# A decoder step on one core: 14 of 17 tiles of h transposed by VectorE out of a reload instead of by TensorE, and the first expert block gathered whole and transposed by TensorE

## What is computed

```python
h = layer_norm(ALPHA * x + mix)            # mix = concat(attn, conv) @ w_out + b_out
lg = h @ w_rg                              # 4 groups, top-1
le = h @ w_re                              # 8 experts in the group, top-2
y_moe = sum over 2 experts of gate * (silu(h @ w1[e]) * (h @ w3[e])) @ w2[e]
y = layer_norm(ALPHA * h + y_moe)
```

## Time and profile before

| | us |
|---|---|
| median of 3 runs (lowest, highest) | 1392.42 (1391.33, 1398.35) |
| profiled execution, its own time | 1402.51 |
| its span in the trace | 1400.6 |
| TensorE matmul busy in the span | 1297.0 (93%) |
| VectorE busy | 684.6 (49%) |
| ScalarE busy | 553.8 (40%) |
| GpSimd busy | 477.0 (34%) |
| output stage, first `turn_h` to last | 599.5 to 866.7 |
| expert matmuls | 906.9 to 1337 |

### The profile page before, as it was taken

The page is one execution under the profiler, slowest core; times in us unless marked ns, Lnnn a source line. Parts: engine busy times, 40 slices in busy tenths (PEclk is TensorE's granted clock), DMA queues, the critical chain, the costliest instruction groups (busy, mean ns, idle before and its releaser), DMA issues.

```text
span 1400.6 us, 21325 instructions
## 1 busy us (share of the span) xinstructions
PE 1297.0 (93%) x5597; PEld 624.9 (45%) x5598; DVE 684.6 (49%) x2065; ACT 553.8 (40%) x895; POOL 477.0 (34%) x643
## 2 busy tenths in 40 slices
PE   8999999989999988899999999999999999999910
PEld 3444445556666655355555555433333333333300
DVE  2424343554556555466666665334444444444338
ACT  0000001434345433333334431166655666566544
POOL 5113110000000000355555543344666566666312
PEclk9999999999999998999999999999999999999955
DMA  6364543222211183345555331259989999999676
GB/s 257 107 210 147 168 128 103 95 75 69 76 68 54 53 251 118 116 184 181 181 181 152 121 114 62 76 157 323 324 261 370 345 283 328 332 370 347 188 241 275
DMA packets 81938, 262.31 MB, mean 187 GB/s; under 512 B 13648, under 2 KB 32656, under 8 KB 68726
## 3 DMA queue, kind: packets, MB, share of 16 engines
q1 hardware_dynamic: 64839, 216.56, 42.6%
q0 software_dynamic: 14192, 41.26, 12.3%
q10 hardware_dynamic: 2823, 3.54, 0.8%
HBM read 202.32 MB, written 63.25 MB: 190 GB/s over the span
## 4 chain that ended last, share of the span: by engine, by line
PE 57%; issue 28%; DMA 6%; DVE 4%; ACT 1%; DVEq 1%; SPq 1%; POOL 1%; POOLq 1%; ACTq 0%
PE P L1017 12%; PE bank_S L1039 10%; PE M L1017 6%; PE P L859 5%; PE bank_S L859 4%; PE bank_S L686 4%; DMA work<-conv_rows 3%; PE P L686 3%; PE P L889 3%; PE bank_T L686 2%; PE M L686 2%; PE M L877 1%; PE M L1025 1%; DMA big<-sum_rows 1%; ACT work L1299 1%
## 5 line engine op out<-in xcount | busy, mean ns | idle before, releaser
L1256 ACT ACTIVATE big<-big 128x2048 f32 x78 | 148.9, 1910 | 161.4 <-issue 102.0
L1018 PE MATMUL P<-big,work 128*64 128x512 f32 x416 | 188.0, 595 | 0.0
L1017 PE MATMUL P<-big,work 128*64 x416 | 188.0, 595 | 0.0
L1900 POOL DMA_INDIRECT work<-h_rows,piece_idx x156 | 150.0, 962 | 77.8 <-issue 55.5
L725 PE MATMUL P<-big,work 128*128 128x256 f32 (+1 forms) x512 | 173.7, 496 | 0.0
L1039 PE MATMUL bank_S<-big,work 128*64 x312 | 142.0, 598 | 3.5 <-ACT big L1262 3.1
L1041 PE MATMUL bank_S<-big,work 128*64 128x512 f32 x312 | 142.1, 598 | 0.0
L1837 POOL TENSOR_SCALAR work<-work 128x1 f32<-128x1 f32 (+1 forms) x17 | 3.8, 223 | 373.9 <-DVE work L1447 373.9
L725 PEld LDWEIGHTS P<-big,work 128*128 128x128 f32 x512 | 97.3, 194 | 70.4 <-issue 63.6
L859 PE MATMUL P<-big,work 128*128 128x512 f32 x256 | 116.0, 607 | 3.2 <-DVE work L1478 3.2
L859 PE MATMUL bank_S<-big,work 128*128 128x512 f32 x256 | 113.3, 595 | 0.0
(11 more groups left out here) (304 smaller groups left out, 2278.7 us busy)
## 6 DMA issues: line engine op xcount, KB each, us to landing
big<-in_w SPq DMA_DIRECT2D x96, 1024.0 KB
work<-in_xt_prompt SPq DMA_DIRECT2D x32, 512.0 KB, 3.5
big<-sum_rows SPq DMA_DIRECT2D x16, 520.0 KB, 8.9
big<-in_toe SPq DMA_DIRECT2D x16, 512.0 KB, 3.5
work<-in_x_prompt SPq DMA_DIRECT2D x16, 512.0 KB, 4.3
h_rows<-work SPq DMA_DIRECT2D x16, 512.0 KB
sum_rows<-work SPq DMA_DIRECT2D x16, 512.0 KB
out_y_prompt<-big SPq DMA_DIRECT2D x16, 512.0 KB
```

The source lines that it names most:

```text
L1017: mm(lower, xgT[j][:, k, 0:U], both[:, k], start=(k == 0), stop=(k == KD - 1))
L1018: last = mm(upper, xgT[j][:, k, U:P], w_up[:, k], start=(k == 0), stop=(k == KD - 1))
L1256: fn(w_up.rearrange("p k m f -> p m k f")[:, :, ks, :], src, ACT.Copy).then_inc(s[f"wu{part}_ok"], 1)
L1900: g.indirect_dma_start(xg[j][:, 256 * i:256 * (i + 1)], None, h_pieces, bass.IndirectOffsetOnAxis(ap=piece_idx[:, j, i // 2, i % 2:i % 2 + ...
```

## The change

Tiles 1 to 14 are no longer transposed by TensorE (tiles 0, 15 and 16 still are: `BY_PE`). SyncE, right behind the two stores of h(c-1), waits until both have landed and until `hT` has been written for the tile before, and reads the tile back in four DMAs, each into 32 partitions of a buffer that is free in this stage (`h_parts`, once `ptB`). VectorE turns it in 32x32 squares straight into `hT` at the head of its iteration, ahead of `route_count`. ScalarE's copy goes for these tiles. The first expert block is gathered by one indirect DMA of whole rows, transposed by eight TensorE transposes into `bank_T` and copied by VectorE; `listed(2)` moves behind that copy; `keep_awake(22)` becomes `keep_awake(14)`.

```diff
+        BY_PE = (0, NT - 1, NT)
+        h_parts = flat_ptB
+            def reload_h(c):
+                tile = OUT_IN[c]
+                sp.wait_ge(s[f"h_out{c % 2}"], 32 * (c // 2 + 1))
+                after(sp, s["hT_ev"], c - 1)
+                src = h_dram[P * tile:P * (tile + 1), :].rearrange("(i t) c -> t i c", t=32)
+                for j in range(4):
+                    sp.dma_start(h_parts[32 * j:32 * (j + 1), :].rearrange("p (i c) -> p i c", i=4),
+                                 src[:, :, 256 * j:256 * (j + 1)]).then_inc(s["hp_in"], 16)
...
                     store_h(c - 1)
+                    if c - 1 not in BY_PE:
+                        reload_h(c - 1)
...
-                if 0 <= c - 1 <= NT:
+                if c - 1 in BY_PE:
                     turn_h(c - 1)
...
-            keep_awake(22)
+            keep_awake(14)
...
+            pe.wait_ge(s["xg_in0"], 16)
+            for k in range(KD):
+                last = tr(T8[:, k, :], xg[0][:, k::KD], ident)
+            last.then_inc(s["pe_hT"], 1)
             for b in range(RING):
                 up(b, b, 0)
...
-                after(act, s["pe_hT"], c)
+                after(act, s["pe_hT"], BY_PE.index(c))
...
-                if 0 <= c - 1 <= NT:
+                if c - 1 in BY_PE:
                     turned_h(c - 1)
...
-                        after(v, s["pe_hT"], c - 2)
+                        after(v, s["pe_hT"], sum(x <= c - 2 for x in BY_PE) - 1)
...
+            def flip_h(c):
+                v.wait_ge(s["hp_in"], 64 * c)
+                after(v, s["pe_ro"], c - 1)
+                nc.vector.transpose(hT.rearrange("p k (i t) -> p i k t", i=4),
+                                    h_parts.rearrange("p (i f k) -> p i k f", i=4, k=KD)).then_inc(s["hT_ev"], 1)
...
             for c in range(NT + 4):
+                if 0 <= c - 2 < NT and c - 2 not in BY_PE:
+                    flip_h(c - 2)
...
-                v.wait_ge(s[f"xg_in{j}"], 64 * (n + 1))
+                v.wait_ge(s[f"xg_in{j}"], 64 * n + (64 if j else 16))
...
-            for b in range(RING):
-                listed(b, b, b, 0)
-            flip_rows(0, 0, 0)
+            listed(0, 0, 0, 0)
+            listed(1, 1, 1, 0)
+            after(v, s["pe_hT"], len(BY_PE))
+            cp(xgT[0].rearrange("p k t -> p (k t)"), bank_T[:, :]).then_inc(s["xgT_ev"], 1)
+            listed(2, 2, 2, 0)
...
-            for b in range(RING):
+            hold_ge(s["tab_ok"], 1)
+            gcp(idx[:, 0:1], own[:, 0, 0:1]).then_inc(s["idx_ok"], 1)
+            hold_ge(s["idx_ok"], 1)
+            g.indirect_dma_start(xg[0], None, h_dram, bass.IndirectOffsetOnAxis(ap=idx[:, 0:1], axis=0)).then_inc(s["xg_in0"], 16)
+            for b in range(1, RING):
                 gather(b, b, b)
```

More of the change, by code:

```diff
@@ L162 @@
 cn_in0 cn_in1 am_in0 am_in1 xr_in0 xr_in1 xb_ok cstat_ok cnm_ok z_ev pe_z zl_ok zs_ok mix_ok
-pe_o0 pe_o1 o0_ev o1_ev lstat_ok lrs_ok dg_ok lz_ok h_ok h_out0 h_out1 sum_out0 sum_out1 pe_hT hT_ev pe_ro ro_ev ro_nm ro_e1 ro_d ro_e2
+pe_o0 pe_o1 o0_ev o1_ev lstat_ok lrs_ok dg_ok lz_ok h_ok h_out0 h_out1 sum_out0 sum_out1 hp_in pe_hT hT_ev pe_ro ro_ev ro_nm ro_e1 ro_d ro_e2
 oh_ok pe_rk rk_ev slot_ok sc_out0 sc_out1 last_out s_cache s_row s_vs
```

## The result

The changed kernel takes 1384.39 us (median of 7 runs, 1378.69 to 1389.57) against 1392.42 (7 runs, 1391.22 to 1398.35): ratio on record 0.991, 95% interval 0.989 to 0.993. By how much is less so: the recorded ratio makes 12.4 us of it, the two medians 8.0 (0.994, outside that interval), and what makes the two differ is not on record. The forecast was 1381.6 in a range of 1374 to 1390; it drew its line for "faster" at 1385.5, and the median lies 1.1 under that line.

What follows compares the result with a forecast made beforehand. TensorE was taken to bound the kernel, nearly tied with VectorE's loop in matrix tiles, and VectorE to be late next. Output stage -6.4 and first expert block -4.4 made -10.8: 1392.4 to 1381.6 us, range 1374 to 1390.

Steps and rivals of the forecast that it cites:

- Read-back, cost zero: SyncE, output stage: the tile read back lands before VectorE asks for it, covered by 2.6 us.
- The held operation: VectorE, output stage: the transpose pushes L1558 (L1581 after) under GpSimd's bias_h, which holds it until T + 7.87.
- T: Output stage: the start of add_half(c, 1) on VectorE, from which times within a tile are counted.
- P: Output stage: the period from tile to tile, 17.28 us before, forecast 16.92 without and 17.05 with a matrix load.
- rival A: Output stage: nothing is held, TensorE sets every period at 16.33; 1374.4 us in all, chance 0.16.
- Matrix tiles: Output-stage tiles that also load a matrix (c = 1 to 9): P = 17.05, tiles 2 to 10 shorter by 3.1 us.
- lateness argument: Matrix tiles: conv_stats, delayed by 3.67 us in any case, absorbs the mean wait of 3.25 for convolution rows.
- rival B: Matrix tiles: waits for convolution rows do not shrink, P stays 17.44 there; 1384.7 us in all, chance 0.15.
- First block: First expert block: fewer dummies and a whole-row gather let up(0) start at 902.5 for 906.92, -4.4 us.
- rival D: First expert block: after idle time up(0) runs its first 6 us mostly at 1.2 GHz, losing 3; 1384.6, chance 0.13.
- rival E: Expert stage: its weight loads set it and both gains are lost again, 0 to -3 us, 1390; chance 0.08.
- Rival C: Output stage: the read-back lands late and VectorE waits for it; 1395 us at its bound, chance 0.10.

Runs made afterwards that it cites:

- e4: The changed kernel with VectorE's transpose of h moved behind route_slot; 0.9885 of the time of the kernel before the change.
- e7_conv_first: The changed kernel with VectorE's transpose of h behind route_slot and each matrix load behind the convolution load; 1375.90 us, 0.9841 of the kernel before.
- e3: The kernel before the change with 28 dummy instructions instead of 44, gather in quarters as before; 0.9997 of the kernel before.
- e5: The changed kernel with keep_awake(6) in place of keep_awake(14), 12 dummies for 28; 0.9900 of the kernel before.
- e8: The changed kernel with the read-back moved to the end of SyncE's step, behind attention, x and matrix loads; 1486.91 us, 1.064 of the kernel before.
- e9_dummies12: e7_conv_first with keep_awake(12) in place of keep_awake(14), 24 dummies; 0.9834 of the kernel before the change.
- e2_block: The kernel before with only the first expert block's part of the change, all 17 tiles still transposed by TensorE; 0.9944 of the kernel before.

## Why the prediction was right

The steps are taken one by one, since a sum can come out for the wrong reasons; two of these did not go as forecast, the last two tiles and what the dummies are worth.

*Read-back, cost zero.* Right. No flip waited. L, from the issue of the first store to the last landing, is about 8, the lower bound that the prediction gave: stores issued from 771.98, reads issued 775.98 to 777.72, landing 2.8 at the median (2.4 to 5.0), where the prediction took 4.3 from a row of the same form and arrived at 10. SyncE waits for the stores 43.5 us in 14 times, 3.5 at most, and nothing that it holds back is late in a tile without a matrix. In the matrix tiles the prediction had nothing to say about the order of `load_conv` behind the matrix; there e4 and e7_conv_first found 16 us of waits, worth 2.7 us of the stage.

*The held operation.* Right, nearly to the digit: L1581 was to end at T + 7.87 and ends at T + 7.88; conv_stats was to start at T + 8.52 and starts at T + 8.38, 0.50 behind it for 0.65; from there to the next T are 8.37 for 8.40. P = 16.75 for 16.92, 16.81 in the mean of the four tiles behind them. e4 shows the cause, so rival A, in which nothing is held, falls by experiment, and its 16.33 for TensorE alone is measured at 16.40.

*Matrix tiles.* P = 16.91 for 17.05 (612.09 to 747.39 for eight). The lateness argument against rival B held: the delay, 3.53 for the 3.67 of the forecast, swallowed nearly all waits; two were left with 5.0 us, 4.4 of them at 603.88, ahead of the first flip.

*Sums.* Tiles 2 to 10 lost 4.2 us (forecast 3.1), 10 to 14 0.9 (0.4), the last two 2.0 (2.9). The last term is the one whose mechanism was missed. I had TensorE set those two periods, since conv_stats is gone from them. Yet T goes from 814.63 to 831.62, 16.99:

```profile
820.58 1.93 DVE L1581 CUSTOM_DVE_ANT_0 route<-work,route 128x32 f32<-128x32 f32 x1
...
822.63 2.18 DVE L1583 CUSTOM_DVE_ANT_0 route<-work,route 128x32 f32<-128x32 f32 x1
...
820.12 2.34 POOL L1896 TENSOR_TENSOR work<-work,lnx 128x1024 f32<-128x1024 f32 x1 [1.32 <-ACT work L1166]
822.42 2.34 POOL L1882 TENSOR_TENSOR work<-work,lnx 128x1024 f32<-128x1024 f32 x1
```

With no convolution tile to wait for, GpSimd runs its two whole-tile adds back to back, and two small operations of VectorE are held, one by each (2.18 ends at 824.81, the add at 824.76). The error of 0.9 us is hidden in the sum by the two others, which were low by 1.1 and 0.5: here the sum came out closer than its terms, which is luck.

*First block.* 14.6 us from the first dummy to `up(0)`, forecast 14.7. -4.5 for -4.4. The pieces fit too: the transposes began 12.12 us after the first dummy, and from their end to `up(0)` were 1.40 for 1.5. Here a step was incomplete though its number came out: "the dummies are the bound" was true for where `up(0)` starts, but not for what it is worth. e3 took the same dummies away with the old gather and gained nothing. What the new gather and the TensorE transposes seem to do is to make the block come early enough and to split the idle time (8 transposes, then 1.41) so that the clock holds. That is my reading of single traces: the clock held behind 1.41 and 1.72 and fell behind 1.98 without transposes, but no run changed the split alone. The fall was rival D, and it was real: it happened in e3 and e5, not in the change.

*Expert stage.* It shifted whole, 405.9 us for 406.5 (rival E falls). *Rival C* did not happen in the change; e8 gives its mechanism a place, one queue entry further down.

Output stage -7.1 for -6.4 (by the starts of `add_half`), block -4.5 for -4.4, sum -11.6 for -10.8. The 2.8 us between median and forecast are within the spread of the runs. The trace is the better witness for the sum, since the two figures for the whole, 8.0 and 12.4 us, lie on either side of 10.8.

## What to carry to other kernels

When work moves to an engine with slack, what counts is not its own duration but which operations it pushes under another engine's long instruction. Look for the order in which the moved work itself is the one that overlaps: here the same 2 us put conv_stats off by 3.5 in one place and by 1.8 in the other. After each bound that falls, read the waits again in the kind of tile that had them: the next one here was two lines of the load order, worth nothing alone and 2.7 us behind the first. And a warm-up row in front of a late input should end just as the input lands; both sides of that point cost, and a shorter row alone can lose at the clock what it wins at the start.

The version that comes out, e7_conv_first or e9_dummies12 (the runs cannot tell these two apart), takes 0.984 and 0.983 of the time before, against 0.991 for the change as it was made.

## What was not expected of the hardware

- A second small operation can be held in the same tile: 1.93 and 2.18 us for two operations of 0.18, each until one GpSimd add ended.
- A 128x1024 transpose on VectorE and a 128x1024 add on GpSimd overlap at full speed: 2.06 and 2.37, 2.04 and 2.35 apart.
- Reads of 128 KB into 32 partitions landed in 2.8 us at the median (56 of them, 2.4 to 5.0) when issued as soon as 1 MB of stores had landed; in e8, where in the matrix tiles they are issued behind 1 MB of matrix, in 6.5.
- What TensorE did ahead of a fall of its clock: 1.98 us of idle time in one piece ahead of `up(0)` were followed by a granted clock of 0.66 (half of the matmuls at the length of 1.2 GHz); 1.72 in e2_block and 1.41 in the changed kernel and in e9_dummies12, behind 1 us of transposes, were not. These are single profiled executions, and the fall at 872 in the kernel before shows that it can also come without a long idle time.
